# An FFN by token halves, with one level of Strassen's method on its input product

## The reference, cut to what matters

```
x  = x + gate1 * (mixed @ w_out)                        # output projection, 1024 x 1024
h  = modulate(rmsnorm(x, norm2_g), shift2, scale2)
a, b = split(h @ w_in)                                  # input product, 1024 x (2 * 2816)
x  = x + gate2 * ((silu(a) * b) @ w_out_ffn)            # output product, 2816 x 1024
```

## Time and profile before

| | |
|---|---|
| three runs | 2883.59 us median (2881.03 to 2883.85) |
| profiled execution, from first to last instruction | 2879.4 us |
| PE busy | 2758.2 us (96%) |
| weight loads (PEld) | 2631.3 us (91%) |
| DVE, ACT, POOL busy | 1310.5, 809.1, 762.2 us (46, 28, 26%) |
| mean granted TensorE clock | 0.991 of full |

### The profile page before, as it was taken

The page is one execution under the profiler, slowest core; times in us unless marked ns, Lnnn a source line. Parts: engine busy times, 40 slices in busy tenths (PEclk is TensorE's granted clock), DMA queues, the critical chain, the costliest instruction groups (busy, mean ns, idle before and its releaser), DMA issues. The chain is left out here.

```text
span 2879.4 us, 40403 instructions
## 1 busy us (share of the span) xinstructions
PE 2758.2 (96%) x16584; PEld 2631.3 (91%) x16584; DVE 1310.5 (46%) x2136; ACT 809.1 (28%) x1268; POOL 762.2 (26%) x332
## 2 busy tenths in 40 slices
PE   7998888999999999999999998899999999999997
PEld 5997677999999999999899997569999999999997
DVE  7798886753222222222558514644532222222224
ACT  4113666251111111111542232542501111111113
POOL 0672123531111111111422122435311111111112
PEclk9999999999999999999999999999999999999999
DMA  6543102411111111100235434324101111111101
GB/s 248 179 147 95 23 16 81 161 65 38 44 44 44 44 44 44 44 31 32 101 103 197 153 120 176 128 81 152 74 30 44 44 44 44 44 44 44 41 3 66
DMA packets 58301, 227.15 MB, mean 79 GB/s; under 512 B 7440, under 2 KB 18128, under 8 KB 47696
## 3 DMA queue, kind: packets, MB, share of 16 engines
q1 hardware_dynamic: 56608, 225.12, 22.3%
q10 hardware_dynamic: 1584, 0.51, 0.1%
HBM read 191.52 MB, written 29.88 MB: 77 GB/s over the span
## 5 line engine op out<-in xcount | busy, mean ns | idle before, releaser
L219 PE MATMUL ps<-hh,wi_hi 128*128 128x384 f32 x2112 | 707.9, 335 | 5.3 <-DVE hid L1354 5.3
L221 PE MATMUL ps<-hh,wi_lo 128*128 128x384 f32 x2112 | 705.5, 334 | 0.0
L220 PE MATMUL ps<-hl,wi_hi 128*128 128x384 f32 x2112 | 705.5, 334 | 0.0
L1354 DVE TENSOR_TENSOR hid<-ps,hid 128x384 f32<-128x384 f32 x132 | 73.4, 557 | 982.9 <-ACT hid L1057 982.9
L219 PEld LDWEIGHTS ps<-hh,wi_hi 128*128 128x128 f32 x2112 | 396.4, 188 | 8.1 <-DVE hid L1354 7.3
L220 PEld LDWEIGHTS ps<-hl,wi_hi 128*128 128x128 f32 x2112 | 396.4, 188 | 0.8
L221 PEld LDWEIGHTS ps<-hh,wi_lo 128*128 128x128 f32 x2112 | 396.4, 188 | 0.0
L1057 ACT ACTIVATE hid<-ps 128x384 f32<-128x384 f32 x132 | 64.7, 492 | 1124.9 <-PE ps L221 1124.9
L1186 POOL TENSOR_TENSOR wi_lo<-raw_in,wi_hi 128x2048 fp32r<-128x2048 f32 x44 | 203.0, 4614 | 647.0 <-ACT wi_hi L1047 646.9
L1365 DVE SCALAR_TENSOR_TENSOR x<-ps,mod,x 128x128 f32<-128x128 f32 (+1 forms) x704 | 326.9, 512 | 77.0 <-PE ps L221 72.9
L219 PE MATMUL ps<-hid_hi,wo_hi 128*128 128x384 f32 x1056 | 354.0, 335 | 2.8 <-DVE x L1365 2.7
(11 more groups left out here) (303 smaller groups left out, 4568.0 us busy)
## 6 DMA issues: line engine op xcount, KB each, us to landing
raw_in<-in_w_ffn_in_dram SPq DMA_DIRECT2D x44, 1024.0 KB, 4.8
wmt<-in_w_mod_t_dram SPq DMA_DIRECT2D x56, 512.0 KB, 3.6
raw_out<-in_w_ffn_out_dram SPq DMA_DIRECT2D x22, 1024.0 KB, 4.8
gla_spill<-turn SPq DMA_DIRECT2D x22, 576.0 KB, 4.1
oraw<-in_w_in_odd_dram SPq DMA_DIRECT2D x24, 512.0 KB, 4.5
wmt_odd<-in_w_mod_t_dram SPq DMA_DIRECT2D x24, 512.0 KB, 4.4
x<-in_x_dram SPq DMA_DIRECT2D x8, 1152.0 KB, 10.1
wm<-in_w_mod_dram SPq DMA_DIRECT2D x16, 512.0 KB, 11.7
```

Source lines behind the costliest of these rows:

```text
L219: pe.matmul(acc, w_hi, in_hi, start=first, stop=False)
L220: pe.matmul(acc, w_hi, in_lo, start=False, stop=False)
L221: return pe.matmul(acc, w_lo, in_hi, start=False, stop=last)
L1354: dve.tensor_tensor(hid[:, t], ps[:, 2 * t + 1, 0:CW], hid[:, t], ALU.mult).then_inc(hid_done, 1)
```

## The change: what it does

The FFN now goes over the tokens in two halves of 576 columns, each as two quarters of 288, and over all 22 hidden tiles for each half, so that `i` runs from 0 to 21 in pairs of hidden tiles. For a hidden tile `t` its input weights [a; b] x [upper, lower half of the 8 contraction tiles] and the input [upper, lower] x [quarter 0, quarter 1] are 2 x 2 blocks, multiplied by one level of Strassen's method (Winograd's form) with 7 block products in place of 8. A block product is 4 contraction tiles x 3 parts = 12 matmuls of 288 columns.

- The seven factors of the input (`fac`) are made once for each half (`scale`, `shift`, `first_sum`, `more_sums`, `third_sum`, `factor_high`, `factor_low`).
- The seven factors of the weights are made for each hidden tile and each half: DVE makes four sums (`weight_sums`, `last_sum`), ACT casts seven factors of 512 elements, POOL splits seven.
- The products are put together in PSUM, by running on in a bank that ACT has copied out (`keep`, three copies), and by DVE (`join`, three sums).
- The output product is split and cast in four parts of 512 elements for each pair, again once for each half.
- The last four tiles of the output projection go by quarters: first all for quarters 0 and 1, and the norm and factors of the first half are made beside those of quarters 2 and 3.
- The first half's last norm, or its result, is made and stored during the second half.

PE's loop holds, for each pair, `hidden(i, 0)`, `contract(i - 1)`, `hidden(i, 1)`: 84, 96 and 84 matmuls of 288 columns.

```
+            def hidden(i, t, first=None, after=None):
+                banks = ((4, 7)[t], 5, (4, 7)[t], 6, (4, 7)[t], 5, (4, 7)[t])
+                for j in range(NP):
+                    wait(pe, w_low, i, 14, 7 * t + j + 1)
...
+                    elif j == 2:
+                        wait(pe, snapped, i, 6, 3 * t + 1)
+                    elif j == 4:
+                        wait(pe, snapped, i, 6, 3 * t + 3)
+                    elif j == 6:
+                        wait(pe, joined, i, 6, 3 * t + 2)
...
+            def contract(i, a=0, b=2 * KT):
+                if a == 0:
+                    wait(pe, hid_low, i, 2, 2)
+                    wait(pe, wout_low, i, 4, 4)
+                for n in range(a, b):
+                    wait(pe, added, i, 2 * KT, n - 3)
...
+            def body(i):                                      # PE
+                hidden(i, 0)
+                contract(i - 1)
+                hidden(i, 1)
...
+            def tile(i, t, last=False, outs=()):              # POOL
+                n = (i, 1) if t == 0 else (i + 1, 0)
+                split_in(i, t, 6)
+                for j in range(1, 7):
+                    if j == 3 and 0 in dict(outs):
+                        split_out(dict(outs)[0][0], dict(outs)[0][1])
+                    if not last:
+                        split_in(*n, j - 1)
+                if 1 in dict(outs):
+                    for a, b in dict(outs)[1]:
+                        split_out(a, b)
+            def body(i):                                      # POOL
+                tile(i, 0, outs=((0, (i - 1, 2)), (1, ((i - 1, 3),))))
+                tile(i, 1, outs=((0, (i, 0)), (1, ((i, 1),))))
...
+            def cast_in(i, t, f):                             # ACT
+                wait(act, used, i, 14, 7 * (t - 1) + f + 1)
...
+            def keep(i, t, dst, bank, j):
+                wait(act, used, i, 14, 7 * t + j + 1)
...
+            def tile(i, t, before=True, last=False, outs=(), extra=()):
+                n = following(i, t)
+                keep(i, t, p0, (4, 7)[t], 0)
+                cast_in(i, t, 6)
+                for j in range(1, 7):
+                    if j == 1:   keep(i, t, p1, 5, 1)
+                    elif j == 2: keep(i, t, p02, (4, 7)[t], 2)
+                    elif j == 3: silu(i, t, 0); cast_out(first of outs)
+                    elif j == 4: hidden_high(of the tile before)
+                    elif j == 5: silu(i, t, 1)
+                    if not last: cast_in(*n, j - 1)
+                cast_out(second of outs)
...
+            def weight_sums(i, t):                            # DVE
+                dve.tensor_tensor(sa[:], a21(t), a22(t), ALU.add).then_inc(summed_w, 1)
+                dve.tensor_tensor(a21(t), a11(t), a21(t), ALU.subtract).then_inc(summed_w, 1)
+                dve.tensor_tensor(sb[:], sa[:], a11(t), ALU.subtract).then_inc(summed_w, 1)
+            def last_sum(i, t):
+                wait(dve, w_low, i, 14, 7 * t + 1)
+                dve.tensor_tensor(a11(t), a12(t), sb[:], ALU.subtract).then_inc(summed_w, 1)
+            def tile(i, t, before=True, last=False, aside=None):
+                join(i, t, hid[:, t, 0], 6, p0, 3, 1)
+                last_sum(*((i, 1) if t == 0 else (i + 1, 0)))
+                join(i, t, b2, A, p1, 4, 2)
+                join(i, t, hid[:, t, 1], 5, p02, 5, 3)
+                hidden_low(*((i - 1, 1) if t == 0 else (i, 0)))
+                gates(i, t)
+            def body(i, H):
+                tile(i, 0)
+                adds(i - 1, H, 0, 6)
+                weight_sums(i + 1, 0)
+                adds(i - 1, H, 6)
+                tile(i, 1)
+                weight_sums(i + 1, 1)
```

More of the change, by code:

```diff
@@ L28 @@
 CW = T // NC
+NQ = 4
+QW = T // NQ
+HW = T // 2
 EPS = 1e-6
@@ L1220, in _ @@
-                with pool.Fori(1, N) as i:
-                    body(i)
+                norm.total(pool, 4, 0)
+                norm.total(pool, 4, 1)
+                weights.split(pool, 7)
+                for m in range(5, KT):
+                    norm.total(pool, m, 0)
+                    norm.total(pool, m, 1)
+                factor_low(0, 0)
+                split_in(0, 0, 0)
+                third_sum(0)
+                factor_low(0, 3)
+                for f in range(1, 6):
+                    split_in(0, 0, f)
@@ new lines, in _ @@
+                hidden(1, 0)
+                contract(0)
+                hidden(1, 1)
+                hidden(2, 0)
+                two_means(norm, 2, 2)
+                contract(1)
+                hidden(2, 1, after=norm.logged)
+                with pe.Fori(3, FFN_PAIRS) as i:
+                    body(i)
+                E = FFN_PAIRS
+                contract(E - 1)
+                hidden(E, 0, first=1)
+                hidden(E, 1)
+                hidden(E + 1, 0)
+                contract(E)
@@ new lines, in _, with scales_early @@
+                adds(E - 2, 0, 0, 6)
+                weight_sums(E, 0)
+                adds(E - 2, 0, 6)
+                def scales_early(j):
+                    if j == 0:
+                        for kk in range(4):
+                            scale(1, kk)
+                tile(E - 1, 1, aside=scales_early)
+                hidden_low(E - 1, 1)
+                weight_sums(E, 1)
+                first_sum(1)
+                adds(E - 1, 0, 0, 2)
+                scale(1, 4)
+                scale(1, 5)
@@ new lines, in _ @@
+                with dve.Fori(E + 1, E + 3) as i:
+                    body(i, 1)
+                if odd is None:
+                    for kk in range(KT):
+                        tail.scale_final(dve, 0, 2, kk)
+                with dve.Fori(E + 3, L) as i:
+                    body(i, 1)
+                tile(L, 0)
+                adds(L - 1, 1)
+                if odd is None:
+                    tile(L, 1, last=True)
+                    hidden_low(L, 1)
+                    adds(L, 1)
+                    for q in range(2, NQ):
+                        for kk in range(KT):
+                            tail.scale_final(dve, q, 1, kk)
+                    return
```

1080 lines of the change are left out of this document (642 added, 438 removed).

## The result

| | changed | before |
|---|---|---|
| median | 3271.2 us (3270.4 to 3274.4, 4 runs) | 2882.8 us (2881.0 to 2883.9, 4 runs) |
| profiled execution's span | 3272.2 us | 2879.4 us |
| PE, DVE, ACT, POOL busy | 2788.9, 2032.9, 1240.1, 1650.7 us | 2758.2, 1310.5, 809.1, 762.2 us |

The ratio is 1.1352, 95% interval 1.1336 to 1.1368. The forecast was 3250 us (3050 to 3370): 0.65% under the measured time.

A forecast was written before the change was run, and what follows sets the result against it. PE's stream bounded the FFN before; afterwards PE would wait for POOL's splits. On the span of 2879.4: -96 + 252 + 47 + 61 + 32 + 37 + 12 + 17 + 4 = +366, span 3245, median 3250 us (3050 to 3370).

The forecast's parts named there:

- PE's own work: Matmuls of both layers: fewer input products at 133.2 ns per 288 columns, slightly dearer output projections; -96 us.
- The narrower matmul at 122.5 ns: Rival on PE's stream: 288-column matmuls cost 122.5 ns by the skill's rule, total 3126 us; 2 in 100.
- POOL's chain: Loop: 18 splits end too late, so PE waits 7.0 us before each of 36 contractions; 252 us.
- the lock: Beside hidden tiles: POOL and two-SBUF-input DVE instructions hold each other up, 0.36 us per 512-element split.
- `weight_sums`: In contractions: three DVE sums delay additions, so PE waits 1.3 us, 36 times; 47 us (0 to 60).
- The clock: After each 7 us wait PE runs slowly for a stretch, 1.7 us lost, 36 times; 61 us.
- The sum of a pair: A loop pair was to take 42 to 44 us where PE's work is 35.2.
- The seams: First and last contractions of halves, first factors and layer ends: 32 + 37 + 12 + 17 + 4 us.
- No locks and no clock: Rival: POOL and DVE hardly meet, slow stretches fall into waits, a wait is 4.6 us; 3080 us, 20 in 100.
- A heavier clock: Rival: each wait may cost two slow stretches, 75 us more; 3325 us, 14 in 100.
- POOL keeps up: Rival: POOL's splits end in time, so only PE's work counts; 2798 us, 5 in 100.

The follow-up runs named there:

- e10_rest: e9_first with DVE's first-tile weight sums behind all contraction additions, projection weights ahead of the squares, and final scalings in two fours: 2887.7 us.
- e1_order: Changed kernel with casts and splits of the output weights' last two parts moved right behind the split of the next tile's first factor: 2983.7 us.
- e8_small: Changed kernel with the loops' DVE instructions with two SBUF inputs cut to an eighth or ninth of their columns: 3156.4 us.
- e2_lastsum: Changed kernel with DVE's last sum of weights of the next hidden tile moved behind its second join: 3294.7 us.
- e3_fill: Changed kernel with 44 unused 288-column matmuls in the loops between hidden tile and PE's wait for the contraction's weights: 3217.9 us.
- e4_all: Changed kernel with the edits of e1_order and e2_lastsum, and ACT's cast of the last factor ahead of its first PSUM copy: 3032.8 us.
- e7_ends: e5_late with the three weight sums spread between additions, and each half's last output weights' three remaining parts ahead of the next tile's second factor: 2929.0 us.
- e5_late: e1_order with DVE's last sum of weights, in each pair's first hidden tile, moved behind the contraction's second addition: 2982.6 us.
- e9_first: e7_ends with output weights' last two parts ahead of the next tile's first factor, and ACT's last factor cast ahead of its first PSUM copy: 2927.0 us.

## Why the prediction was right, point by point

- **PE's own work, -96 us.** Right. 288-column matmuls start 0.133 us apart (749 in 100 us in e10_rest, 133.5 ns), and so a pair of e10_rest, 264 matmuls, takes 35.3 to 35.4 us for the 35.2 of the sum. The narrower matmul at 122.5 ns is out, and with it, for this stream, the formula of the Trainium skill (TensorE: Matmul & The Clock Gate, "Back-to-back issue gap"), which the page gives for an isolated matmul.
- **POOL's chain, 252 us.** The cause was right: POOL stands still in each contraction and starts 2.80 us into the tile, which begins at 1038.31 (2.9 predicted), waits 1.56 us for ACT (1.6), loses 3.2 us to the lock (2.6) and ends 27.3 us after its start (26.7). e1_order shows that the place does it and e8_small the lock. But PE waits 5.84 us (6.0 by the distance of the starts) and not 7.0.
- **The join.** This is the step that was missed. I gave PE 0.2 us of other waits; DVE's `last_sum` stands in its queue ahead of the second join and waits for POOL's split of the first factor, and PE waits 1.6 us. It cost nothing in sum, since POOL's wait became shorter by as much: e2_lastsum. 5.84 + 1.62 = 7.46 us for the 7.2 predicted.
- **`weight_sums`, 47 us.** Mis-sized, by the most of all terms of a pair. The gap behind them in a contraction is 0.2 us in the first halves (1079.27 to 1079.60) and less in the second, for 1.3 predicted: some 5 us in all. e3_fill has the same 0.2 us at full clock. They cost more, 0.6 us in e1_order and 1.6 in e4_all, where DVE comes to the contraction late and POOL works beside them.
- **The clock, 61 us.** Right in the mean: 34 slow stretches cost 58 us, 1.7 each, and e3_fill gets 53 back from 32 of them. Not foreseen was the spread, 10 to 25 matmuls behind equal waits.
- **The sum of a pair** was 10.0 us over PE's work and is 9.9: 7.9 in the two hidden tiles with both waits (7.0 in the sum) and 2.0 in the contraction (3.0 in the sum). The join, missed, and `weight_sums`, too dear, cancelled; the agreement to 0.65% is partly luck.
- **The seams.** 102 us predicted; the 378 us more of both FFNs, with 98.8 less of PE's work and 356 in the loops, leave 121. Not foreseen were 10.7 us in the even layer's output projection, of which 7.0 are a wait for the split of its weights behind the squares (gone in e10_rest), and 7.4 us in the odd layer behind `scale_final`. That the quarters of the output projection cost this was not tried by themselves.
- **The rivals.** No locks and no clock (3080): out by e8_small and e3_fill. A heavier clock (3325), with 3.4 us for each wait: out, the dearest of 34 slow stretches cost 2.7 us and the mean 1.7. POOL keeps up (2798): out for this order of work, but e10_rest shows that it holds for another one. I took POOL's lateness for a property of the change; it was one of where two splits stood.

## What to carry to other kernels

Where an engine stands idle in one phase and late in the next, look first at which of its instructions is waited for in a queue and what stands ahead of it that nobody needs yet: moving two splits out of nine was worth 288 us here with no work saved. Waits hide one another: removing one showed a second of about its size or more in e2_lastsum and e7_ends. And an instruction that is moved away from one wait makes another where it lands: in e4_all, e5_late and e9_first. So add up the path, not the list of waits. Look at many passages of a loop before pricing one: the contraction I read the clock from was among the longest of 34. Put DVE work with two SBUF inputs where POOL stands still.

## What was not expected of the hardware

- The same wait of 5.8 us is followed by slow stretches of very different length, 2.4 to 6.0 us; the wait of 3.1 us in the earlier trace rows by 3.4. Behind the join's wait of 1.6 us one matmul comes at the slow distance.
- A slow stretch can be nearly free where the consumer of the products is late itself: in e4_all contractions with 16 slow matmuls take 14.75 us, and those with 2 of them 14.52, as they wait 1.45 us for DVE instead. In the changed kernel it was not free.
- The lock is felt on both sides by unequal amounts: a split of 512 elements loses 0.45 us (1.75 for 1.29), DVE's sum of 512 elements 0.7 to 1.1 us (1.42 to 1.78 for 0.69).
